# FFN gate and up: one 512-column matmul for the high weights, and the halves joined by ScalarE and VectorE

## The reference

```python
def swiglu_ffn(x, w_gu, w_down):
    gate, up = jnp.split(x @ w_gu, 2, axis=-1)     # w_gu: 1024 x 5632
    return (jax.nn.silu(gate) * up) @ w_down       # w_down: 2816 x 1024

x = x + 0.5 * swiglu_ffn(rms_norm(x, norm), w_gu, w_down)
```

## Time and profile before

| | us |
|---|---|
| median of 2 runs | 2602.02 |
| the two runs | 2598.82, 2605.22 |
| span of the profiled execution | 2597.9 |
| TensorE busy in it | 2562.5 |
| VectorE busy | 1787.7 |
| ScalarE busy | 1389.7 |
| DMA, mean over the span | 172 GB/s |

### The profile page before, as it was taken

One profiled execution on the slowest core, in us unless ns is written; L12 is line 12 of the kernel. 1 busy time (PEld: TensorE's weight loads), 2 busy tenths in 40 slices (PEclk: granted clock), 3 DMA queues, 4 the chain that ended last, 5 costly groups with the idle time before them and its releaser, 6 DMA issues.

```text
span 2597.9 us, 56642 instructions
## 1 busy us (share of the span) xinstructions
PE 2562.5 (99%) x21484; PEld 2481.9 (96%) x21484; DVE 1787.7 (69%) x2852; ACT 1389.7 (53%) x2228; POOL 190.8 (7%) x265
## 2 busy tenths in 40 slices
PE   8999999999999999999999999999999999999998
PEld 8998899999998899999999998999999999989998
DVE  7667586667667586767667657776676686677765
ACT  5456556445445755545445555654454465555543
POOL 1001001000000201000000260000000005300000
PEclk9999999999999999999999999999999999999999
DMA  7654245665554354665664543555555545335563
GB/s 272 210 194 138 85 143 181 226 208 188 193 192 158 104 166 142 202 191 176 208 194 158 182 148 105 167 167 193 191 166 188 186 158 173 130 114 179 178 193 114
DMA packets 122830, 445.87 MB, mean 172 GB/s; under 512 B 13688, under 2 KB 14712, under 8 KB 122688
## 3 DMA queue, kind: packets, MB, share of 16 engines
q1 hardware_dynamic: 120816, 436.79, 51.4%
q0 software_dynamic: 1872, 7.11, 0.8%
HBM read 442.79 MB, written 1.05 MB: 171 GB/s over the span
## 4 chain that ended last, share of the span: by engine, by line
PE 93%; DVE 4%; ACT 1%; DMA 1%; issue 0%; SPq 0%; POOL 0%; DVEq 0%; ACTq 0%; POOLq 0%
PE bank L462 92%; DVE w_lo L1508 1%; PE bank L830 1%; DVE x L1623 1%; DVE z L1619 1%; DVE a L1535 0%; DVE score L1559 0%; DVE rstd_x L1527 0%; DMA x<-in_x_dram 0%; DMA heads<-in_heads_dram 0%; ACT score L1304 0%; ACT w_hi L1072 0%; ACT a L1093 0%; DVE rt L1806 0%; DVE rstd_m L1574 0%
## 5 line engine op out<-in xcount | busy, mean ns | idle before, releaser
L462 PE MATMUL bank<-a,w_hi 128*128 128x256 f32 x7472 | 1304.5, 279 | 4.5 <-DVE a L1535 2.7
L1508 DVE TENSOR_TENSOR w_lo<-raw,w_hi 128x1024 fp32r<-128x1024 f32 x829 | 1012.2, 1225 | 201.6 <-ACT w_hi L1072 199.8
L462 PEld LDWEIGHTS bank<-a,w_hi 128*128 128x128 f32 x7472 | 1132.0, 188 | 18.5 <-issue 12.9
L462 PE MATMUL bank<-a,w_lo 128*128 128x256 f32 x3736 | 1035.6, 277 | 0.0
L1072 ACT CAST w_hi<-raw 128x1024 fp32r<-128x1024 f32 x829 | 842.7, 1044 | 51.9 <-DMA raw<-in_stream_dram 48.7
L462 PE MATMUL bank<-b,w_hi 128*128 128x256 f32 x4800 | 839.5, 278 | 2.8 <-DVE w_lo L1508 2.8
L462 PEld LDWEIGHTS bank<-b,w_hi 128*128 128x128 f32 x4800 | 727.4, 188 | 10.6 <-issue 5.7
L462 PEld LDWEIGHTS bank<-a,w_lo 128*128 128x128 f32 x3736 | 702.7, 188 | 0.0
L462 PE MATMUL bank<-b,w_lo 128*128 128x256 f32 x2400 | 664.8, 277 | 0.0
L462 PEld LDWEIGHTS bank<-b,w_lo 128*128 128x128 f32 x2400 | 450.9, 188 | 0.0
L1132 ACT CAST b<-hmid 128x256 fp32r<-128x256 f32 x132 | 53.7, 407 | 393.9 <-PE bank L462 383.5
(11 more groups left out here) (191 smaller groups left out, 1924.3 us busy)
## 6 DMA issues: line engine op xcount, KB each, us to landing
raw<-in_stream_dram SPq DMA_DIRECT2D x829, 512.0 KB, 3.7
z<-in_biasc_dram POOLq DMA_DIRECT2D x6, 512.0 KB, 4.6
z<-in_biasa_dram POOLq DMA_DIRECT2D x3, 512.0 KB, 5.0
x<-in_x_dram SPq DMA_DIRECT2D x2, 512.0 KB, 8.1
v<-in_mem_dram POOLq DMA_DIRECT2D x2, 512.0 KB, 5.7
out_dram<-x SPq DMA_DIRECT2D x8, 128.0 KB, 1.9
con<-in_con_dram POOLq DMA_DIRECT2D x1, 848.0 KB, 6.4
vec<-in_vec_dram POOLq DMA_DIRECT2D x1, 417.0 KB, 5.6
```

The lines of the kernel that those rows point to most:

```text
L462: return nc.tensor.matmul(out, lhsT, rhs, start=start, stop=stop, skip_group_check=shared)
L1508: return nc.vector.tensor_tensor(out, a, hi.bitcast(F32), ALU.subtract)
```

## The change

For groups 2 to 21 of each FFN:

- TensorE, `gate_up`: for each chunk one matmul with the high weights against both halves of the activations at once, 512 columns into the whole bank (columns 0 to 255 W_hi A_hi, 256 to 511 W_hi A_lo), then one with the low weights of 256 columns onto the first half of the bank. Two matmuls and two weight loads a chunk where there were three.
- ScalarE, `half_copy`: after the gate tile and after the up tile it copies columns 256 to 511 of the bank into `z`. In its order the gate copy stands between the high splits of n+4 and n+5, the up copy ahead of `silu`.
- VectorE, `joined`, in the places of `gate_scale` and `up_scale`: wait for that copy, add columns 0 to 255 of the bank and the copied half, wait for the addition, multiply by `r` in SBUF.

The diff, cut to its core:

```diff
                 def gate_up(n, slot, j, J):
                     for part, freed in ((0, gate_read), (1, up_read)):
                         pe.wait_ge(freed, J - 1)
-                        w_tile(n + part, (slot + part) % RING, gate_up_of(j, False)[part], hi, lo)
+                        wait_split(n + part)
+                        out, s = bank[4 + part + 2 * (j % 2)], (slot + part) % RING
+                        for c in range(C):
+                            wh, wl = w_hi[:, s, c * P:(c + 1) * P], w_lo[:, s, c * P:(c + 1) * P]
+                            mm(out[:, 0:2 * T], wh, act_two["a"][:, c, :, :], c == 0, False, True)
+                            last = mm(out[:, 0:T], wl, hi[:, c, :], False, c == C - 1, True)
+                        last.then_inc(tile_mm, 1)
...
+                def half_copy(u, part, n, signal):
+                    act.wait_ge(tile_mm, n + part + 1)
+                    nc.scalar.copy(second_half(u, part), bank[4 + part + 2 * u][:, T:2 * T]).then_inc(signal, 1)
...
                     if splits:
                         splits(0)
+                    half_copy(u, 0, n, gate_half)
+                    if splits:
                         splits(1)
+                    half_copy(u, 1, n, up_half)
                     silu(u, gate_read, J + 1)
...
+                def joined(out, u, part, n, half, H, signal):
+                    dve.wait_ge(tile_mm, n + part + 1)
+                    dve.wait_ge(half, H)
+                    nc.vector.tensor_tensor(out, bank[4 + part + 2 * u][:, 0:T], second_half(u, part), ALU.add)\
+                        .then_inc(half, 1)
+                    dve.wait_ge(half, H + 1)
+                    nc.vector.tensor_tensor(out, out, r, ALU.mult).then_inc(signal, 1)
...
                     if splits:
                         splits(0)
-                    gate_scale(2 + u, n)
+                    joined(sil[:, u, :], u, 0, n, gate_half, H, gate_read)
                     if splits:
                         splits(1)
-                    up_scale(2 + u, n + 1)
+                    joined(hmid[:, u, :], u, 1, n, up_half, H, up_read)
                     product(u, J)
```

More of the change, by code:

```diff
@@ L213, in build, with second_half @@
         causal = con[:, CON["causal"]:CON["causal"] + 384]
+        def second_half(j, part):
+            return z[:, 2 * (j % 2) + part, :]
         def gain(name, c=0):
@@ L224, in build @@
         gate_read, up_read, first_scaled = sem("gate_read"), sem("up_read"), sem("first_scaled")
+        gate_half, up_half = sem("gate_half"), sem("up_half")
         silu_done, hmul_done, hhi_done, hlo_done = sem("silu_done"), sem("hmul_done"), sem("hhi_done"), sem("hlo_done")
@@ L457, in _ @@
             act_of = {"a": (a_hi, a_lo), "b": (b_hi, b_lo)}
+            act_two = {"a": a_two, "b": b_two}
             fresh = {}
@@ L997, in mixer @@
                     act_of["a"], act_of["b"] = act_of["b"], act_of["a"]
+                    act_two["a"], act_two["b"] = act_two["b"], act_two["a"]
                 if kind == "even":
@@ L1667, in step @@
                 def step(u, n, J, splits):
+                    H = J * 2 - 4 * k - 3
                     if splits:
                         splits(0)
-                    gate_scale(2 + u, n)
+                    joined(sil[:, u, :], u, 0, n, gate_half, H, gate_read)
                     if splits:
                         splits(1)
-                    up_scale(2 + u, n + 1)
+                    joined(hmid[:, u, :], u, 1, n, up_half, H, up_read)
                     product(u, J)
```

## The result

The changed kernel takes 2643.52 us (two runs, 2643.49 and 2643.55) against 2602.02 before: a ratio of 1.0161, with a 95% interval of 1.0116 to 1.0206. It is slower, by 41.5 us, where I had forecast 38 us of gain; two runs on each side cannot tell whether that is more than 2%.

A forecast was written before the change was run, and what follows sets the result against it. TensorE's matmul stream was taken as the bound. Savings of 25.1 us in fast blocks, 7.8 in FFN 6's gate and up and 2.1 in its down blocks gave 2597.9 + 0.9 - 35.0 = 2564 us, range 2552 to 2580.

The forecast's parts named there:

- The bound: Whole kernel: TensorE, busy 2562.5 of 2597.9 us, sets the time, so a cut there counts in full if others keep up.
- (1): Gate and up, groups 2 to 21: one 512-column matmul replaces two of 256; with FFN 6's recovery, 35.0 us saved.
- the 256 columns hide inside it: FFN matmul stream: alternating weight loads and matmuls set the 113.3 ns pitch, hiding the 256 columns' own time.
- 215.5 ns for the 512-column matmul: Gate and up: with its load hidden, the long matmul costs only its stream; with the short one, 328.8 ns.
- 110 + 3 ns: FFN matmul stream: a matmul starts 0.11 us after its load, the next load with it; claimed to make the 113.3 ns.
- the sign that I had named: FFN loops: the forecast is wrong if a 512-column matmul takes more than 227 ns, or TensorE waits for w_lo or hlo.
- The 227 ns that I had put down as the upper bound: Gate and up: bound for one 512-column matmul, taken as two of today's 256-column ones.
- Rival C: FFN loops: changed rhythm locks in the slow pitch, short matmuls 117.8 ns, down tiles 353.3 ns; 2594 us, chance 0.12.
- The sum's 7.8 + 2.1 us: FFN 6: 7.8 us from 320 gate and up blocks, 2.1 from 160 down blocks, if its stream returns to the fast pitch.
- Parts (2) and (3): VectorE's joins, about 0.9 us each, and ScalarE's copies, 0.8 us a group, fit in idle time and cost nothing.
- D: FFN groups: VectorE becomes the bound through waits in each join; 2788 us at 2.0 us a join, chance 0.04.
- The two pitches: FFN loops: 113.3 ns a matmul usually, 117.8 in FFN 6, at the same granted clock; one loop differs by 6.38 us.

The follow-up runs named there:

- the bursts: Kernel before, with series of matmuls of several widths, types and load sizes behind its last tile; fp32r 512 columns took 0.233 us, bf16 0.216; no kernel time given.

## Why the prediction was wrong

- **The bound** was right: TensorE's stream sets the time, and a change in its pitch arrived one for one.
- **The step that failed** is in (1): "the 256 columns hide inside it", and from that 215.5 ns for the 512-column matmul. I had read the load's start beside the matmul's start and taken the 110 + 3 ns for the cause of the pitch. It is a real chain, 112 ns, but it lies beside a stream that costs 113.3 or 117.8 by itself. In the bursts 128 columns are bound by the load and 256 in the slow pitch are not, since half a load leaves them at 0.119. No burst has half loads in the fast pitch; there the evidence is the first 512 columns of FFN 1, which took 226 ns, twice 113.3, with their load hidden. So what the change removed, one load in three, could give nothing in the fast pitch either. With 0.235 a matmul the sign that I had named, more than 227 ns, came true.
- **The plain fp32 rows misled me.** Their 216 ns are two cycles a column, and I used them for a stream of one cycle a column. I had misread the rows as well: the 14 records come from seven matmuls (`keep_going(7)`), so a plain fp32 matmul of 256 columns takes 0.43 us, four cycles a column. The 227 ns that I had put down as the upper bound were the better value, and not even a bound: it was 235.6.
- **The rule beside it.** The Trainium skill (TensorE: Matmul & The Clock Gate, Back-to-back issue gap) has N / 2.4 + 2.5 ns. The bf16 bursts agree, 109 and 216 ns for 256 and 512 columns; the fp32r ones do not, 113 to 118 and 226 to 236.
- **Rival C had the right mechanism and a wrong size.** The slow pitch locked in, on all eight FFNs. I had priced it at 2594 because I let the long matmul keep its 215.5; with 235.6, a block of gate and up is 353.3 ns like one of down. Seven loops of 482 blocks then cost 13.3 ns a block more, 45 us, where the spans differ by 43.8. I gave it 0.12, on the ground that seven FFNs of eight were fast. That counted chance events; it should have asked what the new matmul does to the state of the stream.
- **The sum's 7.8 + 2.1 us** for bringing FFN 6 back to the fast pitch rested on "the long matmul breaks the locked sequence". A single one does break it, as FFN 6 and 7 of the kernel with one 512-column matmul show. But it breaks a fast one as well, and 320 of them in turn with 256-column ones left every loop slow, 170.16 to 170.27.
- **Parts (2) and (3) held.** The joins alone cost nothing (ratio 1.0002), and D fell. One group of VectorE in the changed kernel, the idle time before an instruction in brackets:

```profile
1802.24 0.42 DVE L1672 TENSOR_TENSOR hmid<-bank,z 128x256 f32<-128x256 f32 x1 [0.72 <-ACT z L1149]
...
1805.03 0.43 DVE L1528 TENSOR_TENSOR b<-hmid,b 128x256 fp32r<-128x256 f32 x1 [0.31 <-ACT b L1145]
1805.98 1.23 DVE L1528 TENSOR_TENSOR w_lo<-raw,w_hi 128x1024 fp32r<-128x1024 f32 x1 [0.53 <-ACT w_hi L1085]
1807.82 0.42 DVE L1672 TENSOR_TENSOR sil<-bank,z 128x256 f32<-128x256 f32 x1 [0.62 <-ACT z L1149]
```

It still idles 2.2 us a group, against 2.8 before. The joins add (1936.3 - 1787.7) / 160 = 0.93 us of work a group.

- **The two pitches** I had read rightly from FFN 6, and then used only for the baseline. That the two runs lay 6.40 us apart, just one loop's worth, was luck: the many runs since lie at all distances.

What stays open is what the two states are. The granted clock is 1.00 in both, and both appear with all other engines idle. The runs show what moves the stream from one state to the other at given places, not why.

## What to carry to other kernels

Before you count on a hidden load becoming a gain, measure the same matmul where the load can't bind: a burst of other widths and another type at the end of the kernel costs one run and decides it. If a stage shows two pitches at the same clock, ask of every change of a matmul's shape which pitch it leaves behind, for one instruction can set the pace of the next 1400. The order of long and short matmuls is a knob of its own, worth 33 us between two orders here; neither beat the kernel before.

## What the runs showed of the hardware

- An fp32r matmul behind its own weight load costs 0.443 or 0.460 ns a column at the full granted clock (256 columns 113.3 or 117.8 ns, 384 columns 177, 512 columns 226 to 236), where bf16 shows 109 and 216 ns for 256 and 512 columns.
- The two pitches are states of the stream that a regular sequence keeps, over 1400 matmuls. One 512-column matmul among 256-column ones changed the state in eight FFNs of eight, six times to the slow one and twice to the fast one. A plain fp32 matmul of 8 or 256 columns among them left a fast stream fast and made a slow one fast (five times in three profiles).
- A plain fp32 matmul leaves two records in the trace, 216 ns apart at 256 columns, and takes 0.43 us.
- A 512, 256, 512, 256 order holds the slow pitch (0.353 us a block); 512, 512, 256, 256 takes 0.347, and the 256-column matmuls of the down tiles behind it are then fast (320 x 0.347 + 162 x 0.340 = 166.1, measured 166.0 us a loop).
- On idle engines, 72 matmuls of 256 columns behind plain ones kept the slow pitch to their end (0.353 for three).
- The chain of 128x128 fp32 weight loads runs at 112 ns a load; with loads of 64 columns, matmuls of 128 columns come every 61 ns.
- In the kernel before, a piece of 124 matmuls took 20.95 us with a mean granted clock of 0.77 and 0.66 in its first 6 us and 19.37 us where the clock was 1.00. Where the clock was down, 256 fp32r columns took 213 ns.
